# Gates of branches D and B and the z projection ahead of both branch projections, in a decoder kernel that reads value pages singly

## What is computed

```python
z = xn @ p['w_in']                      # one projection for all branches and gates
o = rmsnorm(o, p['gdn_norm']) * jax.nn.silu(g_z)        # branch B, gated DeltaNet, after a chunked recurrence
gates = jax.nn.sigmoid(gate).reshape(B_, T, N_BRANCH, D_MODEL)
merged = 0.0
for i, o_i in enumerate((o_a, o_b, o_c, o_d)):
    merged = merged + gates[:, :, i] * (o_i @ p['w_branch'][i])
out = merged @ p['w_out']
```

## Time and profile before

| | |
|---|---|
| median of 3 runs | 1864.88 us (1863.91 to 1866.36) |
| the profiled execution | 1866.34 us, of which the span is 1864.6 us |
| PE, busy share of the span | 87% |
| DVE, ACT, POOL | 45%, 30%, 34% |
| mean granted PE clock | 0.918 |
| PE on the chain that ended last | 64%; DVE 18%, ACT 6%, waiting for nothing shown 6%, DMA 3% |

### The profile page before, as it was taken

One profiled execution on the slowest core, in us unless ns is written; L12 is line 12 of the kernel. 1 busy time (PEld: TensorE's weight loads), 2 busy tenths in 40 slices (PEclk: granted clock), 3 DMA queues, 4 the chain that ended last, 5 costly groups with the idle time before them and its releaser, 6 DMA issues.

```text
span 1864.6 us, 28396 instructions
## 1 busy us (share of the span) xinstructions
PE 1618.1 (87%) x11141; PEld 1423.5 (76%) x11141; DVE 839.8 (45%) x1304; ACT 558.1 (30%) x907; POOL 635.3 (34%) x354
## 2 busy tenths in 40 slices
PE   7999899867677778998896899998678999999997
PEld 6898777666656677654443899898577999999996
DVE  4106777678796756223222122225323566663001
ACT  4333233244102222121115333434213333333222
POOL 2237444334466662100000344320402344444341
PEclk9999999888688798999998999999758999999998
DMA  6235223141345433444452522323212222222231
GB/s 198 92 109 176 91 91 96 57 130 57 108 125 180 130 119 97 131 136 131 131 148 87 183 91 81 121 83 113 105 55 68 73 94 95 95 94 71 89 112 48
DMA packets 154389, 200.02 MB, mean 107 GB/s; under 512 B 10180, under 2 KB 112125, under 8 KB 153848
## 3 DMA queue, kind: packets, MB, share of 16 engines
q1 hardware_dynamic: 137253, 169.46, 28.8%
q10 hardware_dynamic: 16011, 24.02, 3.7%
q0 software_dynamic: 992, 4.72, 0.7%
HBM read 187.92 MB, written 10.94 MB: 107 GB/s over the span
## 4 chain that ended last, share of the span: by engine, by line
PE 64%; DVE 18%; ACT 6%; issue 6%; DMA 3%; POOL 2%; ACTq 0%; SPq 0%; DVEq 0%; POOLq 0%
PE pb L775 45%; PE sd L775 17%; ACT ar L1104 3%; DVE ar L1494 3%; PE sd L779 2%; DVE ar L1630 2%; DVE ar L1514 2%; DVE ar L1637 2%; DVE ar L1497 1%; DVE ar L1500 1%; DMA ar<-in_cache_fox_k 1%; POOL ar L747 1%; ACT L1104 1%; ACT wh L1104 1%; DVE ar L1687 1%
## 5 line engine op out<-in xcount | busy, mean ns | idle before, releaser
L736 POOL TENSOR_TENSOR wl<-raw,wh 128x1024 fp32r<-128x1024 f32 (+2 forms) x196 | 427.5, 2181 | 1083.6 <-ACT wh L1104 1082.1
L775 PE MATMUL pb<-xh,wh 128*128 128x260 f32 x2176 | 645.1, 296 | 27.1 <-DVE xl L1494 10.3
L775 PE MATMUL pb<-xl,wh 128*128 128x260 f32 x2176 | 629.5, 289 | 0.0
L775 PE MATMUL pb<-xh,wl 128*128 128x260 f32 x2176 | 628.1, 289 | 0.0
L775 PEld LDWEIGHTS pb<-xh,wh 128*128 128x128 f32 x2176 | 425.3, 195 | 44.5 <-issue 35.6
L775 PE MATMUL sd<-ar 128*128 128x128 f32 (+7 forms) x1584 | 361.4, 372 | 79.9 <-DVE ar L1494 26.3
L775 PEld LDWEIGHTS pb<-xl,wh 128*128 128x128 f32 x2176 | 425.3, 195 | 0.7
L775 PEld LDWEIGHTS pb<-xh,wl 128*128 128x128 f32 x2176 | 424.8, 195 | 0.0
L1104 ACT ACTIVATE wh<-raw 128x1024 fp32r<-128x1024 f32 (+2 forms) x208 | 201.5, 969 | 582.1 <-PE pb L775 552.6
L775 PEld LDWEIGHTS sd<-ar 128*128 128x128 f32 (+4 forms) x1584 | 209.0, 196 | 199.0 <-issue 136.1
L747 POOL TENSOR_TENSOR ar<-ar 128x512 f32<-128x512 f32 x128 | 179.6, 1403 | 93.0 <-DMA ar<-in_cache_fox_k 62.7
(11 more groups left out here) (173 smaller groups left out, 1703.1 us busy)
## 6 DMA issues: line engine op xcount, KB each, us to landing
raw<-in_w_in SPq DMA_DIRECT2D x40, 1024.0 KB, 5.5
ar<-in_cache_fox_k SPq DMA_DIRECT2D x128, 256.0 KB, 2.7
ar<-in_cache_fox_v SPq DMA_DIRECT2D x128, 256.0 KB, 2.8
raw<-in_w_ffn_in SPq DMA_DIRECT2D x22, 1024.0 KB, 5.0
raw<-in_w_branch SPq DMA_DIRECT2D x16, 512.0 KB, 3.6
raw<-in_w_ffn_out SPq DMA_DIRECT2D x8, 1024.0 KB, 5.3
ar<-in_cache_mem_k ACTq DMA_DIRECT2D x1, 4096.0 KB, 15.8
raw<-in_w_out SPq DMA_DIRECT2D x4, 1024.0 KB, 5.3
```

Of the source, the lines that this page charges most:

```text
L736: pool.tensor_tensor(wl[:, p % 2, 0:kt, :], raw[:, u % 2, 0:kt, half * P:(half + 1) * P], wh[:, p % 2, 0:kt, :].bitcast(F32), SUB).then_in ...
L775: return pe.matmul(o, l, r, start=start, stop=stop, skip_group_check=True)
```

## The change

The pieces' order becomes: A and C as before, then all 8 gate pieces of D, all 8 of B, the 4 of z, and only then the 8 branch pieces of D and the 8 of B. The 16 gate tiles are kept in DRAM meanwhile: ACT stores each after its tanh (`gate_scratch`), and SP loads them back into four buffers `pair4`, which take the place of `pairA` and `pairB`. The mark before `gateD` moves to before `brD`, and the five `gp` steps move behind it. The z factor is no longer multiplied into `oB` at its piece but kept in `oC` and multiplied in during `gp`.

```diff
@@ -101,14 +101,19 @@
         unit("w_in", 0, KD, C_AB + h * 256, "ab", 2 * h)
     for n in range(6):
         unit("w_in", 0, KD, C_GQ + n * 256, "gx", 2 * n)
-    for n, br in enumerate("ACDB"):
-        if br == "B":
-            for h in range(2):
-                unit("w_in", 0, KD, C_GZ + h * 256, "gz", 2 * h)
+    for br in "AC":
         b = "ABCD".index(br)
         for h in range(4):
             unit("w_in", 0, KD, C_GATE + b * D + h * 256, "gate" + br, 2 * h)
             unit("w_branch", b * BD, KB, h * 256, "br" + br, 2 * h)
+    for br in "DB":
+        for h in range(4):
+            unit("w_in", 0, KD, C_GATE + "ABCD".index(br) * D + h * 256, "gate" + br, 2 * h)
+    for h in range(2):
+        unit("w_in", 0, KD, C_GZ + h * 256, "gz", 2 * h)
+    for br in "DB":
+        for h in range(4):
+            unit("w_branch", "ABCD".index(br) * BD, KB, h * 256, "br" + br, 2 * h)
     for h in range(4):
         unit("w_out", 0, KD, h * 256, "wo", 2 * h)
     for h in range(4):
@@ -174,8 +179,8 @@
         + [("gdn", n, 0) for n in range(12, 18)]
         + [("dc", n) for n in range(3)] + [("ds", n) for n in range(4)] + [("VSTART",)]
         + [("gdn", n, c) for c in range(1, 4) for n in range(-1, 18)]
-        + [("gp", n) for n in range(5)]
-        + [("PAGES",), ("df", 0), ("df", 1)] + [("BEFORE", "gateD")]
+        + [("PAGES",), ("df", 0)] + [("df", 1)] + [("BEFORE", "brD")]
+        + [("gp", n) for n in range(5)] + [("BEFORE", "brB")]
         + [("ex", n) for n in range(6)] + [("ml", n) for n in range(4)] + [("BEFORE", "wo")]
         + [("AFTER", "cq")]
         + [("xm", n) for n in range(3)] + [("x", n) for n in range(XU + 3)] + [("xd", n) for n in range(4)]
@@ -251,7 +256,11 @@
 
     for p in range(NP_):
         kind = PIECES[p][3]
-        if p == first_piece(kind) and ("BEFORE", kind) in SIDE:
+        if kind == "brD" and p == first_piece(kind):
+            evac(p - 2)
+            through(("BEFORE", kind))
+            out.append(("split", "brD"))
+        elif p == first_piece(kind) and ("BEFORE", kind) in SIDE:
             through(("BEFORE", kind))
         if kind in ("wo", "kv", "co", "fg", "fo") and p == first_piece(kind):
             evac(p - 1)
@@ -270,7 +279,7 @@
         for h in range(2):
             at_piece[0] = p - 1 + h
             out.append(("piece", p, h))
-            if kind in ("gateC", "gateB", "gateD") and p == first_piece(kind) and h == 0:
+            if kind in ("gateC", "brB") and p == first_piece(kind) and h == 0:
                 evac(p - 1)
                 out.append(("split", "br" + kind[-1]))
             step(p)
@@ -495,6 +504,8 @@
         sd = ps("sd", [P, 4, 512])
         s0, s1, s2, s3 = (sd[:, n, :] for n in range(4))
 
+        pair4 = v(PR, 4, T)
+        gscr = nc.dram_tensor("gate_scratch", (2, KD, P, T), F32, kind="Internal").ap()
         xscr = nc.dram_tensor("x_scratch", (P, KD * T), F32, kind="Internal").ap()
         vscr = nc.dram_tensor("v_scratch", (NB * FH * (512 + FD),), F32, kind="Internal").ap()
         qscr = nc.dram_tensor("q_scratch", (NB, 512), F32, kind="Internal").ap()
@@ -510,6 +521,7 @@
         qb_in, xs_out, xs_in, qs_out = sem("qb_in"), sem("xs_out"), sem("xs_in"), sem("qs_out")
         out_sem = sem("out_sem")
         stg_out = [sem(f"stg_out{n}") for n in range(2)]
+        gate_out, gate_in = [sem(f"gate_out{n}") for n in range(2)], [sem(f"gate_in{n}") for n in range(4)]
         ss_in, ss_out, mv_in = sem("ss_in"), sem("ss_out"), [sem(f"mv_in{n}") for n in range(2)]
         pool_c, act_c, dve_c = stage("pool_chain"), stage("act_chain"), stage("dve_chain")
         pool_made = stage("pool_made")
@@ -686,10 +698,24 @@
             sp.wait_ge(pt_in, 32)
             for i in range(3):
                 page("cache_fox_k", i)
+            def gate(g):
+
+                if g == 0:
+                    for s in range(2):
+                        sp.wait_ge(gate_out[s], 16 * KD)
+                    sp.wait_ge(ev_all.sem, count(dve_tile, mt_of("gz")))
+                if g >= 4:
+                    sp.wait_ge(mt_dve.sem, mt_d[mt_of("brD", 0) + g - 4])
+                sp.dma_start(pair4[:, g % 4, :], gscr[g // KD, g % KD]).then_inc(gate_in[g % 4], 16)
+
             for e in TIMELINE:
                 if e[0] == "piece" and e[2] == 1 and PIECES[e[1]][1] == 0 and PIECES[e[1]][0] + 2 < len(UNITS):
                     unit(PIECES[e[1]][0] + 2)
-                elif e[0] == "k" and e[1] + 3 < N_PAGE:
+                if e[0] == "piece" and e[2] == 1 and PIECES[e[1]][3] in ("brD", "brB"):
+                    g = e[1] - first_piece("brD")
+                    for i in range(g + 2 if g else 0, min(g + 3, 2 * KD)):
+                        gate(i)
+                if e[0] == "k" and e[1] + 3 < N_PAGE:
                     if e[1] >= 1:
                         sp.wait_ge(page_free.sem, e[1])
                     page("cache_fox_k", e[1] + 3)
@@ -1143,6 +1169,12 @@
                     fn(fs[:, j, :], pb[:, m % 2, 1, TH - NB:TH], ACT.Copy, mt_act, scale=c)
                 elif kind == "cv":
                     fn(both(pairA[:, s, :]), x, ACT.Copy, mt_act, scale=0.5)
+                elif kind in ("gateD", "gateB"):
+                    g = (0 if kind == "gateD" else KD) + idx
+                    if g >= 2:
+                        act.wait_ge(gate_out[s], 16 * (g // 2))
+                    fn(both(pairB[:, s, :]), x, ACT.Tanh, mt_act, scale=0.5)
+                    act.dma_start(gscr[g // KD, idx], pairB[:, s, :]).then_inc(gate_out[s], 16)
                 elif kind == "cg" or kind.startswith("gate"):
                     fn(both(pairB[:, s, :]), x, ACT.Tanh, mt_act, scale=0.5)
                 elif kind in ("gx", "fg"):
@@ -1153,6 +1185,7 @@
                 elif kind == "ac":
                     fn(both(pairA[:, s, :]), x, ACT.Copy, mt_act)
                 elif kind == "gz":
+                    act.wait_ge(gate_out[s], 16 * KD)
                     fn(both(pairA[:, s, :]), x, ACT.Copy, scale=0.5)
                     fn(both(pairB[:, s, :]), x, ACT.Tanh, mt_act, scale=0.5)
                 elif kind == "kv":
@@ -1572,11 +1605,15 @@
                         stt(both(xT[:, idx, :]), both(pairB[:, s, :]), 1.0, x, ADD, MUL, mt_dve)
                         cp(fl8[:, 0:1], fl8[:, 1:2], ev_all)
                     else:
-                        stt(both(tmp), both(pairB[:, s, :]), 1.0, x, ADD, MUL, mt_dve)
+                        g = pairB[:, s, :]
+                        if kind != "brC":
+                            n = (0 if kind == "brD" else KD) + idx
+                            g = pair4[:, n % 4, :]
+                            dve.wait_ge(gate_in[n % 4], 16 * (n // 4 + 1))
+                        stt(both(tmp), both(g), 1.0, x, ADD, MUL, mt_dve)
                         tt(xT[:, idx, :], xT[:, idx, :], tmp, ADD, ev_all)
                 elif kind == "gz":
-                    stt(pairA[:, s, :], pairB[:, s, :], 1.0, pairA[:, s, :], ADD, MUL)
-                    tt(oB[:, idx, :], oB[:, idx, :], pairA[:, s, :], MUL, ev_all)
+                    stt(oC[:, idx, :], pairB[:, s, :], 1.0, pairA[:, s, :], ADD, MUL, ev_all)
                 elif kind in ("wo", "co", "fo"):
                     if kind == "wo" and idx == 0:
                         dve.wait_ge(xs_in, 16)
@@ -1701,7 +1738,8 @@
                             out=t, in0=t, scalar=P ** -0.5 if n <= 2 else 1.0, in1=lrs2[:, j, :], op0=MUL, op1=MUL))
                 elif kind == "gp":
                     dve.wait_ge(a2v.sem, av + 1)
-                    stt(oB[:, n - 1, :], oB[:, n - 1, :], col(V_GN), lrs, MUL, MUL, dve_s)
+                    stt(oB[:, n - 1, :], oB[:, n - 1, :], col(V_GN), lrs, MUL, MUL)
+                    tt(oB[:, n - 1, :], oB[:, n - 1, :], oC[:, n - 1, :], MUL, dve_s)
                 elif kind == "gdn":
                     c = s[2]
                     cc = slice(c * P, (c + 1) * P)
```

## The result

The changed kernel took 1870.1 us in the median of 20 runs (1861.18 to 1879.95), the kernel before 1864.62 in 20 runs beside them (1859.67 to 1870.17). The ratio is 1.0028, interval (95%) 1.0015 to 1.0041: slower by 0.28%, some 5 us, a little over the 0.2% from which I count a difference. The profiled execution's span is 1868.8 us.

The account below looks back on a forecast made before the run. PE was taken to bound the whole, the recurrence steps' latency about 80 us in part. -7.6 + 14.1 - 3.0 = +3.5 on the profiled 1866.34 gave 1869.8; less 1.46 for the median, rounded, 1868.5 us, range 1857 to 1880.

Parts of the forecast that it names:

- The gate stretch: Run of recurrence steps with D, B gate and z half pieces between: covered idle time saves 7.6 us (0 to 18.4).
- the four waits: PE waits behind pages 47, 63, 79 and 111, ACT copying out before the step: 10.3 us in all, forecast to stay.
- The run's end: Last recurrence matmuls through last pages, `df` and normalisation to the exports: plus 14.1 us, between plus 9 and plus 18.
- The pages: Last sixteen pages, standing alone: 1.1 us apart from the fifth on, the sixteenth done at 20.5 us (17.3 to 22.7).
- the clock's rival: Slower: PE at 1.2 GHz from the last page to B's first piece, plus 11 us, 1880; chance 0.16.
- the round's chain of 5.76: Each normalising step's wait between matmuls: 5.05 us as before, with table loads, plus 0.71 for the added DVE product.
- the upper bound's three conditions: For plus 18 us at the run's end: pages at 1.3 us, all sums at 1.2 GHz, `df` blocked by POOL.
- Behind it: From the exports through the branch pieces of D and B up to `wo`: minus 3.0 us together.
- The stalls of 1.00: Six PE stalls, each at a gate pair behind a branch pair, go: minus 6.0 us.
- the case that I had priced at 4.6 in place of 3.3: Split of B's input without a gate piece beside it: plus 3.3 us, or 4.6 if POOL's split blocks DVE.
- the four waits go: Faster rival: PE's four waits behind 16 pages vanish too, another 10.3 us and about 3 of half clock, 1855; chance 0.15.
- Memory rows and gates at once: Slower rival: memory rows load beside gates and could take twice their 4.91 us, 1873; chance 0.17.

Follow-up runs that it names:

- both edits: Changed kernel with ACT's copy after each 16 pages put behind the recurrence step and the normalisation put back beside the last sixteen pages: 1852.9 us, ratio 0.9933.
- PE filled: Changed kernel with idle matmuls into a free bank during PE's waits in the normalisation and for the memory rows: 1869.5 us, ratio 1.0016.
- by the pages with three edits: Changed kernel, normalisation beside last pages, ACT's copy behind the step, one activation table, sums not waiting for DVE's products: 1841.9 us, ratio 0.9882.

## Why the prediction came out as it did

**The time** was forecast at 1868.5 and measured at 1870.1, inside the range; but I gave the largest chance to no change, and the measurement is slower by more than 0.2%. My sum of +3.5 lay 0.2 us below that bound, so that any term decided it. That the time came so near is in part luck: between the two profiled executions the stages differ by 7.5 us and not by 3.5, and the part ahead of them, which the change does not touch, was 3.0 shorter in the execution after.

**The gate stretch**: -7.6 forecast, -8.5 measured, with the four waits where the text put them, 10.2 us. That ACT's copy ahead of the step is their cause is shown: with the copy behind it, nothing of them is left in the changed kernel.

**The run's end**: +14.1 forecast, +17.6 measured, near the upper bound of 18. Two terms of this step were mis-sized. The pages: I took 1.1 us from one to the next, between 0.9 and 1.3. From the fifth (1081.26) to the sixteenth (1094.94) they are 1.24 apart in the mean, though single steps lie above my upper value, the last three at 1.40 to 1.44. The last page ends 21.9 us behind the start of the recurrence's last matmuls, not 20.5. And the clock: I took the sums at 1.2 GHz in every second round; they were so in all (2.07), which is 1.9 us more. This is the part of the clock's rival that came true; its larger part, half clock under the exports, did not come: D's halves took 1.68 there. The rest held: 5.01 us through DRAM, `df` in 1.6, the round's chain of 5.76 (7.85 - 2.07 = 5.78). Two bounds of this step were wrong sums: with 0.9 from page to page the last page ends at 18.3, not 17.3, which makes plus 10 of the lower bound of plus 9; and the upper bound's three conditions make 14.1 + 2.2 + 1.9 + 1.5 = 19.7, not 18.

`df`'s first operation took 0.21 us with POOL idle, where it took 1.69 beside POOL's split. The same two engines met again further on, at DVE's addition to `xT` ahead of the split of B's input:

```profile
1101.36 0.21 DVE L1527 TENSOR_TENSOR ar<-ar 64x32 f32<-64x32 f32 x1 [23.17 <-PE sd L805]
...
1170.35 1.79 DVE L1527 TENSOR_TENSOR xT<-xT,ar 128x520 f32<-128x520 f32 x1
...
1170.32 1.26 POOL L762 TENSOR_TENSOR wl<-raw,wh 128x512 fp32r<-128x512 f32 x1 [8.89 <-ACT wh L1130]
```

**Behind it**: -3.0 forecast, -1.5 measured. The stalls of 1.00 are gone; the kernel before had seven of them (from 1034.03 to 1177.80), not six, so that this term gave 7.0 and the others cost some 2.5 more than I priced. The wait ahead of the memory rows' transposes is 8.01 (some 8 forecast). B's input costs the 4.36 of the wait, and 1.79 in place of 0.71 in front of it is the case that I had priced at 4.6 in place of 3.3; the memory rows' two scalings on DVE took 2.42 instead of 1.54, with a split of POOL beside the second. The rest was not taken apart.

**The rivals.** That the four waits go was wrong. Memory rows and gates at once: the rows landed in 4.97 us (1151.54 in the chain), and without the gates' traffic the ratio was the same. PE did not wait for `gate_scratch`; in three of the other runs (both edits, PE filled, by the pages with three edits) its wait ahead of `wo` was 1.2 to 1.6 us longer, with a gate's load in the chain.

What my reading passed over: the rounds' table loads stood in the earlier trace rows, and I costed them as given. They are the largest part of a round that was taken out. That they alone made the new place of the normalisation dear is not shown, since they were worth 8.2 us in the old place too.

## What to carry to other kernels

A chain of short operations on two engines that is moved from beside slow work to beside short pieces can cost almost its own length, so its rounds are to be shortened before it is moved; look in it first for table loads and for waits on results that the next step does not read. Where an engine idles, then drains a result, then starts what others wait for, put the drain behind that start. And a pace read from two or three transfers is not that of a dozen: here the rows of before gave 0.9 and 1.3, the last bare pages 1.44, and the mean that set the time was 1.24.

## What the runs showed of the hardware

Logarithm and exponential in turn cost a table load of 1.28 us each time, eight in the normalisation; with a set that holds both, loaded once, their own times stayed (0.70 and 0.65) and all eight loads left the rounds. PE's clock went from 0.69 to 0.92 over the rounds by idle matmuls alone, and from 0.69 to 0.84 by shorter waits without any:

```profile
1101.84:1124.84 23.00, 16.90 (x93) 15.46 (x93) 10.95 (x16) 13.51 (x22) 4.07 (x3) 0.84 0.36 115
```
